# Weight sums for the seven-product down projections, formed in device memory by GpSimd's adding DMAs and loaded as ring slabs; six of eleven slabs by seven products

## What is computed

```python
def swiglu_2(h, w_in, w_out):
    gate, up = jnp.split(h @ w_in, 2, axis=-1)
    return (jax.nn.silu(gate) * up) @ w_out

def second_block(x, ...):
    for l in range(DEPTH):                       # DEPTH = 2
        x = x + 0.5 * swiglu_2(rms_norm(x, ffn1_norm[l]), ffn1_w_in[l], ffn1_w_out[l])
        h = rms_norm(x, mix_norm[l]) @ w_mix_in[l]
        ...
        x = x + y @ w_mix_out[l]
        x = x + 0.5 * swiglu_2(rms_norm(x, ffn2_norm[l]), ffn2_w_in[l], ffn2_w_out[l])
    return x
```

## Time and profile before

| | us |
|---|---|
| median of three executions (lowest, highest) | 1645.88 (1645.65, 1646.16) |
| profiled execution, its own time | 1645.73 |
| its span (first to last instruction) | 1644.4 |
| PE busy | 1619.5 |
| DVE busy | 1225.9 |
| ACT busy | 850.4 |
| POOL busy (its issuing of DMAs included) | 291.6 |

### The profile page before, as it was taken

One profiled execution on the slowest core, in us unless ns is written; L12 is line 12 of the kernel. 1 busy time (PEld: TensorE's weight loads), 2 busy tenths in 40 slices (PEclk: granted clock), 3 DMA queues, 4 the chain that ended last, 5 costly groups with the idle time before them and its releaser, 6 DMA issues.

```text
span 1644.4 us, 21147 instructions
## 1 busy us (share of the span) xinstructions
PE 1619.5 (98%) x7872; PEld 1309.0 (80%) x7872; DVE 1225.9 (75%) x1476; ACT 850.4 (52%) x1062; POOL 291.6 (18%) x429
## 2 busy tenths in 40 slices
PE   6999999999999999999999999999999999999999
PEld 3776788887778888788888878888888888888887
DVE  3898778897777664766978775678667978866686
ACT  3436654435575443645656554454544647564453
POOL 0001000000002240134303002450044204003350
PEclk9999999999999999999999999999999999999999
DMA  9784398897548876577565428766676664337661
GB/s 351 240 291 166 108 317 280 310 359 254 203 124 270 272 249 204 174 224 232 193 190 175 129 86 246 219 196 221 200 215 212 212 193 163 106 128 234 214 211 52
DMA packets 250295, 346.22 MB, mean 211 GB/s; under 512 B 16160, under 2 KB 197124, under 8 KB 250192
## 3 DMA queue, kind: packets, MB, share of 16 engines
q1 hardware_dynamic: 236288, 323.00, 59.7%
q0 software_dynamic: 11472, 17.34, 4.5%
q10 hardware_dynamic: 2432, 4.51, 0.8%
HBM read 329.32 MB, written 1.05 MB: 201 GB/s over the span
## 4 chain that ended last, share of the span: by engine, by line
PE 90%; DVE 5%; ACT 3%; DMA 1%; issue 1%; SPq 0%; DVEq 0%; ACTq 0%
PE bank L491 21%; PE bank L493 21%; PE bank L492 21%; PE bank L898 5%; PE bank L899 5%; PE bank L903 5%; DMA raw<-in_ada_w 1%; PE bank L846 1%; PE bank L1411 1%; PE bank L1412 1%; PE bank L1414 1%; DVE lo L2057 1%; PE bank L1219 1%; PE bank L517 0%; DVE ST L2419 0%
## 5 line engine op out<-in xcount | busy, mean ns | idle before, releaser
L2057 DVE TENSOR_TENSOR lo<-raw,hi 128x2048 fp32r<-128x2048 f32 x230 | 527.8, 2298 | 194.4 <-ACT hi L1467 194.2
L1467 ACT ACTIVATE hi<-raw 128x2048 fp32r<-128x2048 f32 x242 | 461.9, 1913 | 248.1 <-PE bank L493 173.0
L491 PE MATMUL bank<-hi,XTh 128*128 128x512 f32 (+1 forms) x1424 | 558.8, 392 | 1.6 <-DVE XTl L2214 1.2
L493 PE MATMUL bank<-hi,XTl 128*128 128x512 f32 (+1 forms) x1424 | 551.4, 387 | 0.0
L492 PE MATMUL bank<-lo,XTh 128*128 128x512 f32 (+1 forms) x1424 | 550.9, 387 | 0.0
L491 PEld LDWEIGHTS bank<-hi,XTh 128*128 128x128 f32 x1424 | 267.4, 188 | 65.7 <-issue 12.3
L493 PEld LDWEIGHTS bank<-hi,XTl 128*128 128x128 f32 x1424 | 267.4, 188 | 55.3
L492 PEld LDWEIGHTS bank<-lo,XTh 128*128 128x128 f32 x1424 | 267.6, 188 | 53.8 <-issue 1.0
L3151 POOL DMA_DIRECT2D HTR<-BLK x320 | 192.4, 609 | 626.5 <-DVE BLK L2645 586.5
L898 PE MATMUL bank<-hi,HTh 128*128 128x512 f32 x400 | 156.6, 392 | 0.0
L899 PE MATMUL bank<-lo,HTh 128*128 128x512 f32 x400 | 155.7, 389 | 0.0
(11 more groups left out here) (420 smaller groups left out, 1860.1 us busy)
## 6 DMA issues: line engine op xcount, KB each, us to landing
raw<-in_ffn_w_in SPq DMA_DIRECT2D x176, 512.0 KB, 4.9
raw<-in_ffn_w SPq DMA_DIRECT2D x132, 512.0 KB, 5.0
raw<-in_ada_w SPq DMA_DIRECT2D x96, 512.0 KB, 5.4
raw<-in_ffn_w_out SPq DMA_DIRECT2D x88, 512.0 KB, 4.1
raw<-in_w_mix_in SPq DMA_DIRECT2D x52, 512.0 KB, 4.6
raw<-in_od_pw_w SPq DMA_DIRECT2D x24, 512.0 KB, 5.7
HTR<-BLK POOLq DMA_DIRECT2D x240, 48.0 KB, 4.0
raw<-in_ev_w_in SPq DMA_DIRECT2D x20, 512.0 KB, 9.5
```

The costliest lines, as they stand in the source:

```text
L491: pe.matmul(dst, xh, wh, start=start, stop=False)
L493: return pe.matmul(dst, xl, wh, start=False, stop=stop)
L1467: act.activation(hi[r][:, :], raw[g % RAW][:, :], ACT.Copy).then_inc(*up("hi", d))
L2057: dve.tensor_tensor(lo[r][:, :], raw[g % RAW][:, :], hi[r][:, :].bitcast(F32), ALU.subtract).then_inc(*up("lo", d))
```

## The change

The weight sums of a fast slab are no longer made by DVE and ACT from the loaded slab. A new function `weights_sums(p)` in GpSimd's queue forms them in device memory, in tensors `sums{p}`, with DMAs that copy and DMAs that add to their destination. It works on batches of two slabs, three batches for an FFN. SP loads each sums tensor slab like any other slab of the ring (`sums_slab`, right behind the fast slab, whose unused quarter is no longer loaded: `fast_slab`), ACT and DVE split it like any other slab, and `seven` takes the sums from the ring slot behind the fast slab's own. `FASTS` grows from four to six slabs. Signs in the column sums and shared sums change with the form of the sums; column sums go in three batches of two slabs; `shared_sums` moves behind the loop of splits.

```diff
-FASTS = (1, 3, 5, 7)
+FASTS = (0, 1, 3, 4, 6, 7)
...
+    def fast_slab(w, s):
+        def parts(slot):
+            d = slot[:, :].rearrange("p (k n) -> p k n", k=2)
+            return [(d[:, 0, 0:512], w[2 * s * P:(2 * s + 1) * P, 0:512]), (d[:, 1, :], w[(2 * s + 1) * P:(2 * s + 2) * P, :])]
+        add(parts)
+
+    def sums_slab(p, i):
+        def parts(slot):
+            return [(slot[:, n * D:(n + 1) * D], A["sums"][p][i, :, n * D:(n + 1) * D]) for n in range(2)]
+        add(parts)
...
+            def weights_sums(p):
+
+                l, kind = (p - 3) // 3, "ffn1" if p in (3, 6) else "ffn2"
+                w = A[f"{kind}_w_out_2"][l, :, :].rearrange("(s k p) n -> s k p n", k=2, p=P)
+                for n in FAST_BATCH:
+                    own = FAST_BATCH[n]
+                    s0 = FASTS[own[0]]
+                    v = A["sums"][p][own[0]:own[-1] + 1, :, :]
+                    k0, k1 = w[s0:s0 + 2, 0, :, :], w[s0:s0 + 2, 1, :, :]
+                    pool.dma_start(v[:, :, 0:D], k0).then_inc(*up("sums_part", (p, n, 0), 16))
+                    pool.dma_start(v[:, :, D:SLAB], k1).then_inc(*up("sums_part", (p, n, 1), 16))
+                    pool.wait_ge(*at("sums_part", (p, n, 1)))
+                    pool.dma_start(v[:, :, 0:512], k0[:, :, 512:D], accum_op=ALU.add).then_inc(*up("sums_part", (p, n, 2), 16))
+                    pool.dma_start(v[:, :, 512:D], k1[:, :, 512:D], accum_op=ALU.add).then_inc(*up("sums_part", (p, n, 3), 16))
+                    pool.wait_ge(*at("sums_part", (p, n, 3)))
+                    pool.dma_start(v[:, :, D + 512:SLAB], v[:, :, 0:512], accum_op=ALU.add).then_inc(
+                        *up("sums_part", (p, n, 4), 16))
+                    pool.wait_ge(*at("sums_part", (p, n, 4)))
+                    pool.dma_start(v[:, :, D:D + 512], v[:, :, D + 512:SLAB], accum_op=ALU.add).then_inc(
+                        *up("sums_made", (p, n), 16))
+                    pool.wait_ge(*at("sums_made", (p, n)))
...
                 pool.dma_start(WB[o:o + HD, g // 2, o:o + HD], A["ev_fourier_w"][0, g, :, :]).then_inc(*up("four_w", g, 16))
+            weights_sums(3)
             pool.wait_ge(*at("o_full", 3))
...
             pool.dma_start(ZA[PERIOD:PERIOD + 1, :, :, :], A["conv_bias"]).then_inc(*up("conv_in", 3, 16))
+            weights_sums(5)
             move_blocks(2)
...
+                weights_sums((6, 8)[l])
                 move_blocks(3 * l + 5)
...
-                        if freed in fast_at:
-                            sp.wait_ge(*at("t_sum", fast_at[freed]))
+                if split in sums_at:
+                    sp.wait_ge(*at("sums_made", (sums_at[split], fast_batch(fast_at[split - 1][1]))))
```

In `seven`, the waits for `t_hi` and `t_lo` go, and the sums come from the ring slot q behind the slab's own slot r:

```diff
                 def w_sum(n):
-                    return TH[:, n * 512:(n + 1) * 512], TL[:, n * 512:(n + 1) * 512]
+                    return hi[q][:, n * 512:(n + 1) * 512], lo[q][:, n * 512:(n + 1) * 512]
...
-                pe.wait_ge(*at("t_hi", (f, i)))
-                pe.wait_ge(*at("t_lo", (f, i)))
...
+                ready(d + 1)
+                three(bank[3][:, :], *x_sum(0), *w_sum(0), begin, end)
```

More of the change, by code:

```diff
@@ L120, in weight_slabs @@
 def weight_slabs(A):
-    slabs, first, dense = [], {}, []
+    slabs, first, dense, fast_at, sums_at = [], {}, [], {}, {}
     up0 = 2 * len(COLS5) + len(DOWN0)
@@ L442, in program @@
         TR = tile_at("TR", [P, SLAB], tmp_at)
[L443 to L447, removed]
+        SR = tile_at("SR", [P, 8, 4, P], tmp_at)
+        SL = tile_at("SL", [P, 8, 4, P], tmp_at, F32R)
+        SH = [tile_at(f"SH{n}", [P, 2, 4, P], (gate_at, gate_at + 4096, scr_at)[n], F32R) for n in range(3)]
         SUMS2 = SG[:, :, :].rearrange("p t n -> p (t n)")
@@ L453, in col @@
             return COLS[:, vec[name]:vec[name] + n]
-        slabs, first, dense = weight_slabs(A)
+        A["sums"] = {p: nc.dram_tensor(f"sums{p}", (len(FASTS), P, SLAB), F32, kind="Internal").ap() for p in FAST}
+        slabs, first, dense, fast_at, sums_at = weight_slabs(A)
         quarter_at = {g: key[1:] for key, g in first.items() if key[0] == "ada"}
-        fast_at = {first[f"down{p + 1}"] + s: (FFNS[p], i) for p in FAST for i, s in enumerate(FASTS)}
         def fox_stat(i, o, n):
@@ L467, in mix_columns, with down_at, down_order, fast_batch @@
             return UM[:, t, a:a + 2 * (b - a)].rearrange("p (x n) -> p x n", x=2)[:, :, 0:HALF]
+        def down_at(p, s):
+            return first[f"down{p}"] + s + (sum(x < s for x in FASTS) if p - 1 in FAST else 0)
+        def down_order(p):
+            kinds = [(s, (0, 1) if p - 1 in FAST and s in FASTS else (0,)) for s in range(DOWNS[p][0])]
+            return [(down_at(p, s) + n, s, n) for s, parts in kinds for n in parts]
+        def fast_batch(i):
+            return next(n for n in FAST_BATCH if i in FAST_BATCH[n])
+        def sums_slot(i):
+            return (i + 4) % 8
+        def sums_own(n):
+            i = FAST_BATCH[n][0]
+            return slice(sums_slot(i), sums_slot(i) + len(FAST_BATCH[n]))
         def sums_of(p):
@@ L2528, in residual @@
                 else:
[L2529 removed]
+                    dve.wait_ge(*at("used", down_at(p, DOWNS[p][0] - 1)))
                 if p - 1 in FAST:
@@ L2685, in ffn @@
                     split(d + 2 * c + 1 + RING)
-                    if p in FAST and c == NC - 2:
-                        weights_sums(f, first[f"down{p + 1}"], 0)
                     if p in SHIFTED:
@@ L3204, in sync_engine @@
             sp.dma_start(X[:, :, :], A["x"][0, :, :].rearrange("(t p) d -> p t d", p=P)).then_inc(*up("x_in", 0, 16))
-            for g, (_, parts) in enumerate(slabs):
+            for g, (split, parts) in enumerate(slabs):
                 r = g % RAW
```

182 lines of the change are left out of this document (78 added, 104 removed).

## The result

The changed kernel takes 2440.88 us (median of 4 executions, 2434.37 to 2449.05) against 1646.0 us: a ratio of 1.483, 95% interval 1.481 to 1.485. The direction was as forecast, the size was not: 1972 us had been forecast, 1664 to 2140 as the range. 795 us were lost where 326 were expected.

The account below looks back on a forecast made before the run. PE, busy 98% of the span, was taken to bound the kernel. Losses of 84 (up product of FFN 0) and 92, 79, 79 (moves), less 8 gained, made 326 us on 1645.7: 1972 us, range 1664 to 2140.

Parts of the forecast that it names:

- Two engines: GpSimd's copies and first adds: two DMA engines carry each, at 44.9 GB/s; the forecast case, loads sharing, chance 0.70.
- The exception: GpSimd's direct copies go over all 16 engines whatever the shape; TAPW, with at least twelve engines, agreed with it.
- The cost of one FFN's transfers: GpSimd's three batches per FFN, alone on the engines: 142 to 186 us, with 142 taken.
- the bound of 186: One FFN's transfers in GpSimd's queue if adds run at half rate: 186 us, giving 2143 us in all.
- Sharing with the loads: Moves of FFN 2, 5, 8: transfers use only engine time loads leave free before due times (146.5, 129.1 us); 92, 79, 79 lost.
- The up product of FFN 0: 205 to 328 us: FFN 3's transfers share engines evenly, loads keep 0.56 of their pace, PE loses 84 us.
- The gain: Fast down products on PE: 24 matmuls fewer, 5.4 us, and three stalls gone, 2.5 us; together 7.9 us.
- The later shared sums: Shared sums move behind the split loop, some 3.7 us later; put at nothing, at most 4 x 1 us.
- All sixteen engines: Rival: all sixteen DMA engines carry GpSimd's transfers, 63 to 81 us per FFN, hidden before the moves; 1638 us, chance 0.13.
- Two engines in the gaps: Rival: transfers on two engines leave loads their pace and lose none; only 13 us late twice, 1664 us; chance 0.11.
- The ring of four: Rival: in fast down products two of four ring slots go per slab, 1 us lost in each of 24; 1662 us, chance 0.03.
- the case of nothing: Rival: transfers hidden, but later shared sums and ring take back 5 to 8 us; within 0.2% of 1645.7, chance 0.03.

Follow-up runs that it names:

- rows outermost: The changed kernel with the two copies and two first adds of each batch described with the 128 rows as outermost step: 1670.4 us, 1.0145 of the kernel before.
- the run with FFN 3 alone: The changed kernel with GpSimd's transfers for FFN 3 only, on two engines each; sums of FFN 5, 6 and 8 not computed: 1785.6 us.
- the run without transfers: The changed kernel without GpSimd's transfers; sums slabs loaded from rows of w_out, so sums not computed: 1637.73 us, 0.995 of the kernel before.
- the spread form: The changed kernel, rows outermost, its twelve batches spread over GpSimd's idle stretches; one batch at 137 us: 1650.8 us, or two there: 1655.1 us.
- the best form: Rows outermost, batches spread with two at 137 us, GpSimd waiting for down6's end before the batch ahead of FFN 6's moves: 1639.82 us, 0.9965 of before.

## Why the prediction was wrong in size

**Two engines: right.** The choice between two and sixteen was worth 770 of the 795 us lost, though it does not turn the sign by itself: with rows outermost the kernel is still 1.45% slower than before. That run shows it as a matter of the outermost step: 16.4% of the engines' time against 66.8% (the latter beside loads), with packets of the same size. By the rule that the Trainium skill gives in "DMA: Bandwidth & Descriptors" (Why a DMA increments its semaphore by 16 and not by 1) this is so, and the trace agrees: two slabs against 256 rows gave two engines' time (42.4 us of packets in 21.0), 256 rows against 256 gave 94.6% of sixteen. The exception, which that section gives for some direct copies and TAPW bore out, did not reach these transfers.

**The cost of one FFN's transfers: the step that failed.** "I take 142, since only copies have a row." Measured alone: 334. The three parts, per batch:

| | predicted (with its waits) | measured alone |
|---|---|---|
| two copies | 25.7 | 48.0 |
| two first adds | 14.0 | 48.9 |
| two whole adds | 7.6 | 14.4 |

The time of one copy was right: 23.4 us from the load stage's 22.4 GB/s, and 23.4 us lie between the first two rows of that batch. (That is partly luck: the packets took 21.0 us, 25.0 GB/s an engine.) What was wrong is the word "beside": the copies of a pair went one after another (22 us more). The adds ran at half the copy's rate, which stood in the prediction as the upper bound, and also one after another. Both together are more than the bound of 186, since that had the pairs overlap. Serial issue was never put forward as a case, and it alone takes the time out of the range: 23.4 + 11.7 us more in each of three batches make 247 us where 142 stood, over the 186 that gave the upper bound of 2143. Why GpSimd holds the second one back stays open. An add that reads its destination at no cost was the cheaper of two ends without a row, and I took it for no better reason than that. The whole adds took twice the time that I gave them, 7 us a batch.

**Sharing with the loads: charged too much at the moves.** I let transfers run only in the time that loads leave free, 49.5 of 146.5 us. Measured: the transfers of FFN 5, 6 and 8 took 355, 342 and 341 us with 129 to 146 us of loads beside them, against 334 alone, while PE was busy for 118.92 of 120 us in 1280 to 1400. With two of sixteen engines taken, the loads kept their pace there and the transfers lost 2 to 6%. So the loss per place is nearly the transfers' time less the 146.5 and 129: 355 - 146.5 = 208, 342 - 129 = 213, 341 - 129 = 212; the stalls are 214, 211 and 212. Those due times were right to within 6 us. The two errors have opposite signs and the first is far larger.

**The up product of FFN 0: right number, wrong working.** 84 forecast; 94 late at the end of down1, 86 in the run with FFN 3 alone. But in the up product itself 67 were lost: PE kept 0.68 of its pace and not 0.56, and the transfers stayed beside it for the whole stage and beside down1 behind it, where 27 more went, since they took 412 us. That the number came out near is luck.

**The convolution's constants: missing.** The transfers for FFN 3 also stand ahead of TAPW, TAPD, B and ZA in GpSimd's queue. With 142 us they would have been through; with 412 they held the constants back to 549 us, and 58 more were lost (of these PE waits 48.0 us for TAPD). The prediction listed what stood behind the other three sets and not what stood behind this one.

**The gain: right.** 7.9 forecast, 8.2 in the run without transfers; DVE, ring and loads keep ahead, as worked out. The later shared sums, put at nothing, cost nothing there; beside transfers in the spread form they are where PE stands 9.6 us.

**The sum with the measured terms:** 94 + 58 + 216 + 216 + 219, less the gain of 8 and some 6 that PE wins back behind the last stall: 789 us, the difference of the spans. (The three large terms are the steps of lateness from place to place, with the gain of the down products between them added back; of the first two, what PE wins back behind the stall is already off.)

**The rivals.** All sixteen engines became real with another order of two dimensions, but an FFN's transfers then took 130 to 144 us beside loads and not 63 to 81. So the forecast 1638 us needs also the spreading of batches, and 1640 is what the best form takes. "Two engines in the gaps" was right that the loads keep their pace beside the three later sets, and wrong that they do so in the up product of FFN 0, and 334 us did not fit into the gaps. The ring of four never bound, and the case of nothing fell with the cost of the transfers. That a contention can sit in a fast down product, where 301 GB/s were wanted against 359, was waved away there; it is where the spread forms lost 12 and 10 us.

## What to carry to other kernels

Before a transfer between two regions of device memory is put into a queue, look at the outermost step on both sides: here it decided whether two or sixteen engines carried it, and the order of two dimensions was worth 770 us. A queue that waits inside its own work delays all that stands behind it, so list every later entry, with its due time, for each place where work is inserted, and put no more new work into a gap than the slack behind it holds. And place it by the load of the stretch that it lands in: the same 40 us batch was free in the mixers, where loads hold 0.34 of the DMA engines, and cost 14 us where they hold 0.98.

## What the runs showed of the hardware

A copy over two engines is accompanied by some 1800 packets of 4 bytes, 2064 in all, where the sixteen-engine form has 272. Whole two-engine transfers of a pair ran one after another, except the two copies that open each FFN's set; half copies ran beside each other, half adds mostly not. An adding transfer moves 12.3 GB/s on an engine (128 packets of 2 KB in 21.3 us) where a copy moves 25.0 (128 of 4 KB in 21.0). The size of the packets does not explain it: a 2 KB packet of an add takes 184 ns on the mean, one of the loads, into SBUF, 95 ns (205 to 328 in the run without transfers).

The stalls are long enough for PE's clock. In the kernel before it was granted in full throughout; here, in 695 to 900, with PE busy for 18 us of 205, the mean is 0.56, and PE restarts at the lower of its two levels, 1.2 GHz, after 214 us of idle time. PE's timeline at the restart, and stretches around it (columns as in the earlier trace rows):

```profile
927.19 0.79 PE L529 MATMUL bank<-hi,XTh 128*128 128x512 f32 x1 [214.05 <-DVE HID L2678]
...
928.20 0.63 PE L531 MATMUL bank<-hi,XTl 128*128 128x512 f32 x1
928.63 0.63 PE L529 MATMUL bank<-hi,XTh 128*128 128x512 f32 x1
```

```profile
900.00:915.00 15.00, 0.00 (x0) 0.00 (x0) 0.00 (x0) 0.00 (x0) 4.74 (x8) 0.50 0.39 52
925.00:935.00 10.00, 7.81 (x28) 6.34 (x29) 9.86 (x12) 7.72 (x10) 4.26 (x7) 0.75 0.43 122
935.00:945.00 10.00, 10.00 (x46) 8.28 (x45) 9.93 (x12) 3.74 (x4) 2.43 (x4) 1.00 1.08 321
```

Starts are 0.43 us apart there and back at 0.23 once the clock is granted in full, before 935; that is under 2 us a stall, little beside the 214. In the up product of FFN 0 it counts for more: PE waits there again and again (seven waits, up to 15.7 us), the mean granted clock of 205 to 328 is 0.86, and a matmul's share of the busy time is 0.239 us (91.87 for 385) where it was 0.217, by estimate 8 of the 67 us lost in that stage.
